# Mixture-of-experts layer: two 64-row expert visits replaced by full 128-row visits of the loop

## What is computed

```python
def moe_swiglu(h, router, w_gate, w_up, w_down):
    probs = softmax(h @ router)
    top_p, top_i = lax.top_k(probs, TOP_K)          # TOP_K = 2
    top_p = top_p / sum(top_p)
    combine = sum(one_hot(top_i, N_EXPERTS) * top_p[..., None])
    a = einsum('bsd,edf->bsef', h, w_gate)          # 8 x 1024 x 1408
    u = einsum('bsd,edf->bsef', h, w_up)            # 8 x 1024 x 1408
    hid = silu(a) * u * combine[..., None]
    return einsum('bsef,efd->bsd', hid, w_down)     # 8 x 1408 x 1024
```

## Time and profile before

| | us |
|---|---|
| median of three runs | 1987.22 |
| the three runs | 1984.53, 1987.22, 1990.09 |
| the profiled execution, its own time | 1985.19 |
| its span in the trace | 1983.4 |

### The profile page before, as it was taken

How to read it: one execution, slowest core, us unless ns; L and a number is a source line. 1 busy time by engine, 2 the same in 40 slices (tenths; PEclk the granted TensorE clock), 3 DMA queues, 4 the chain that set the end, 5 groups by cost and what they waited for, 6 DMA issues and landing times.

```text
span 1983.4 us, 32235 instructions
## 1 busy us (share of the span) xinstructions
PE 1850.1 (93%) x13940; PEld 1553.6 (78%) x13940; DVE 1014.3 (51%) x1302; ACT 797.5 (40%) x1116; POOL 269.0 (14%) x245
## 2 busy tenths in 40 slices
PE   4999899999989999998999899999998989899994
PEld 2889789888878999887888798887877447367884
DVE  1955344454635344326944445545638234157885
ACT  2444632222534322215364522225345243246774
POOL 2510032332000000004400123330002000000001
PEclk9998889999988999998989999999998999999997
DMA  9461142122652334327621223117555986969994
GB/s 343 175 224 49 43 160 94 58 86 86 224 190 89 124 127 127 128 106 275 230 100 48 116 88 108 44 46 253 205 202 182 379 309 240 378 213 320 372 380 151
DMA packets 186386, 350.70 MB, mean 177 GB/s; under 512 B 5097, under 2 KB 60417, under 8 KB 185744
## 3 DMA queue, kind: packets, MB, share of 16 engines
q1 hardware_dynamic: 182464, 335.03, 47.7%
q0 software_dynamic: 3792, 13.77, 2.0%
HBM read 319.41 MB, written 29.36 MB: 176 GB/s over the span
## 4 chain that ended last, share of the span: by engine, by line
PE 81%; DMA 6%; DVE 4%; ACT 4%; SPq 2%; issue 1%; POOL 0%; POOLq 0%; DVEq 0%; ACTq 0%
PE bank L1101 5%; PE bank L1653 5%; PE bank L1622 5%; PE bank L1330 5%; PE bank L1623 4%; PE bank L1625 4%; PE bank L1103 4%; PE bank L1102 4%; PE bank L1513 3%; PE bank L1511 3%; PE bank L1512 3%; PE bank L1137 3%; PE bank L1139 3%; PE bank L1138 3%; PE bank L1055 2%; DMA ring<-in_ada_w 2%
## 5 line engine op out<-in xcount | busy, mean ns | idle before, releaser
L1103 PE MATMUL bank<-hT_hi,ring_split 128*128 128x384 f32 x576 | 195.8, 340 | 0.0
L1759 ACT ACTIVATE ring_split<-ring 128x1024 fp32r<-128x1024 f32 (+2 forms) x84 | 119.5, 1441 | 177.2 <-DMA ring<-in_ffn_w_up 103.8
L2620 DVE TENSOR_TENSOR ring_split<-ring,ring_split 128x2048 fp32r<-128x2048 f32 (+1 forms) x28 | 73.9, 2671 | 141.8 <-ACT ring_split L1759 141.8
L1101 PE MATMUL bank<-hT_hi,ring_split 128*128 128x384 f32 x384 | 142.3, 371 | 4.3 <-DVE modv L2294 2.9
L1139 PE MATMUL bank<-ring_split,hT_hi 128*128 128x256 f32 x480 | 137.2, 286 | 0.0
L720 DVE TENSOR_TENSOR ring_split<-ring,w_upper_a 128x1536 fp32r<-128x1536 f32 (+2 forms) x54 | 96.5, 1814 | 76.3 <-PE bank L1653 68.1
L1102 PE MATMUL bank<-hT_lo,ring_split 128*128 128x384 f32 x384 | 130.4, 340 | 0.0
L1653 PE MATMUL bank<-ring,hT 128*64 128x256 f32 (+1 forms) x592 | 109.7, 510 | 17.9 <-DMA ring<-in_moe_w_up 13.9
L1513 PE MATMUL bank<-hT_hi,ring_split 128*128 128x384 f32 x352 | 118.8, 337 | 0.0
L1511 PE MATMUL bank<-hT_hi,ring_split 128*128 128x384 f32 x352 | 117.6, 334 | 0.0
L1512 PE MATMUL bank<-hT_lo,ring_split 128*128 128x384 f32 x352 | 117.2, 333 | 0.0
(11 more groups left out here) (423 smaller groups left out, 4539.3 us busy)
## 6 DMA issues: line engine op xcount, KB each, us to landing
ring<-in_w_in SPq DMA_DIRECT2D x28, 2048.0 KB, 8.9
ring<-in_ada_w SPq DMA_DIRECT2D x24, 2048.0 KB, 12.8
ring<-in_moe_w_gate SPq DMA_DIRECT2D x32, 1024.0 KB, 7.7
ring<-in_moe_w_up SPq DMA_DIRECT2D x32, 1024.0 KB, 10.0
ring<-in_moe_w_down SPq DMA_DIRECT2D x16, 1536.0 KB, 9.0
ring<-in_w_branch SPq DMA_DIRECT2D x8, 1536.0 KB, 12.8
ring<-in_ffn_w_gate SPq DMA_DIRECT2D x11, 1024.0 KB, 5.4
ring<-in_ffn_w_up SPq DMA_DIRECT2D x11, 1024.0 KB, 7.9
```

The source lines that it names most:

```text
L1101: mm(out, hi, hT_hi[:, k], start=k == 0, stop=False)
L1103: last = mm(out, lo, hT_hi[:, k], start=False, stop=k == KT - 1)
```

## The change

The small visits go. `VISITS` becomes V0 = (0, None), V1 = (1, 0), V2 = (2, 1): every expert has an item of 128 slots, and ranks 1 and 2 have a side of 64 slots besides. Ranks 3 to 7 are items 3 to 7, all in the loop. `N_SIDE` becomes 2, `N_FIX` 8, `NI` 16; `FIRST` stays 3. The loop's body is the same.

Since no small visit stands ahead of a wide one now, slots 0 and 1 of a side are put behind products 8 and 9 of the item visit before it (`wide_next`), in V0 and in V1. V0's load of rows (`rows_load(0)`) fetches the rows of item 1 and of side 0 instead of side 0 alone, and V0 transposes both. The semaphore counts (`slots`, `sides_before`) follow.

The core of the diff:

```diff
-VISITS = ((0, None), (None, 0), (1, 1), (None, 2), (2, 3))
+VISITS = ((0, None), (1, 0), (2, 1))
...
-BY_RANK = ((0, None), (1, 1), (2, 3), (3, None), (4, None), (5, None), (None, 2), (None, 0))
+BY_RANK = ((0, None), (1, 0), (2, 1), (3, None), (4, None), (5, None), (6, None), (7, None))
...
+        def wide_next(v):
+
+            return None not in following(v)
+
+        def sides_before(v):
+
+            return sum(s is not None for _, s in VISITS[:v])
...
         slots = []
-        for item_v, s in VISITS:
+        for v, (item_v, s) in enumerate(VISITS):
+            ahead_v = [(following(v)[1], j) for j in range(2)] if wide_next(v) else []
...
-            elif s is not None:
-                slots += [(s, j) for j in range(2, M_GU + M_DN)]
+            else:
+                slots += ([(s, j) for j in range(2, M_GU + M_DN)] if s is not None else []) + ahead_v
...
+            def rows_load(v):
+
+                n_item, n_side = following(v)
+                if n_item is not None:
+                    sp.wait_ge(ga_mm, 2 * n_item)
+                    sp.dma_start(xs, slot_rows(xslots, n_item)).then_inc(xs_in, 16)
+                if n_side is not None:
+                    if n_side:
+                        sp.wait_ge(side_t, turned("rows", n_side - 1))
+                    side_load(n_side)
...
                 if j == M_SLOT + 1:
                     for done in moved:
                         sp.wait_ge(done, 32)
-                    side_load(0)
+                    rows_load(0)
...
                             if s is not None and j < M_GU + 2:
                                 side_slot(v, j + 2)
+                            elif v is not None and j >= M_GU + 2 and wide_next(v):
+                                side_slot(v + 1, j - M_GU - 2)
...
                         if not last:
                             for j in range(2):
-                                lower(j, i + 1)
+                                lower(j, i + 1, following(v_)[1] if v_ is not None else None)
```

More of the change, by code:

```diff
@@ L646, in build @@
         slots = []
-        for item_v, s in VISITS:
+        for v, (item_v, s) in enumerate(VISITS):
+            ahead_v = [(following(v)[1], j) for j in range(2)] if wide_next(v) else []
             if item_v is None:
-                slots += [(s, j) for j in range(M_GU + M_DN - 1)] + [(s + 1, 0), (s, M_GU + M_DN - 1), (s + 1, 1)]
-            elif s is not None:
-                slots += [(s, j) for j in range(2, M_GU + M_DN)]
+                slots += [(s, j) for j in range(M_GU + M_DN - 1)] + ahead_v[0:1] + [(s, M_GU + M_DN - 1)] + ahead_v[1:2]
+            else:
+                slots += ([(s, j) for j in range(2, M_GU + M_DN)] if s is not None else []) + ahead_v
         def m_place(j, split=False):
@@ L856, in _ @@
                 e = sp.value_load(table[0:1, x:x + 1], min_val=0, max_val=NE - 1)
-                n_item, n_side = following(v)
                 for j in range(M_GU + M_DN):
@@ L867, in _ @@
                             store_out(VISITS[v - 1][0])
[L868 to L873, removed]
+                        rows_load(v)
             with sp.Fori(FIRST, n_items) as i:
@@ L1686, in side_visit @@
                                 side_turn(s, M_BLK - 1)
-                            if j >= M_GU + 2:
+                            if j >= M_GU + 2 and wide_next(v):
                                 side_slot(v + 1, j - M_GU - 2)
@@ L1707, in main_visit @@
                                 pe.wait_ge(side_yt, FG + 2 * N_SIDE)
-                            elif j == 2 and v:
-                                pe.wait_ge(side_yt, FG + 2 * VISITS[v - 1][1] + 2)
+                            elif j == 2 and sides_before(v):
+                                pe.wait_ge(side_yt, FG + 2 * sides_before(v))
                             for h in parts_of(j):
@@ L2176, in side_visit @@
                         gathered(i)
-                        side_rows(n_side)
+                        if n_side is not None:
+                            side_rows(n_side)
                         side_copy(s, 2)
```

## The result

| | before | after |
|---|---|---|
| median, us | 1985.42 (20 runs, 1978.04 to 1991.92) | 1992.6 (20 runs, 1986.28 to 2001.6) |
| ratio of after to before | | 1.0032, 95% interval 1.0021 to 1.0043 |
| span of the profiled execution | 1983.4 | 1999.8 |

The changed kernel is slower by 0.32%, some 6.4 us; the two medians lie 7.2 us apart. The forecast was 1992.5 us, 5.3 us over the 1987.2 us that three runs of the kernel before had given.

The account below looks back on a forecast made before the run. The tensor engine was taken to bound all but the small visits, which were bound by loads. The terms -107.96 + 96.60 + 14.27 + 2.18 + 0.17 = +5.26 us on a 1987.22 us median gave 1992.5 us, range 1986 to 2001.

Parts of the forecast that it names:

- The two visits removed and the two added: Expert stage: dropping small visits V1 and V3 saves 107.96 us; two more loop visits of 48.30 us add 96.60.
- The moved side slots: Ends of V0 and V1: slots 0 and 1 of two sides, four at 3.57 us, nothing hidden, +14.27 us.
- The transposes: V0 and V1: eight more transposes of item rows in each, 1.09 us per group, +2.18 us; copies hidden.
- the list of signs: Expected timeline: loop visits 48.3 us, V1 82.8, V2 74.6, V0 8.3 longer, no PE wait for weights behind V0.
- The seam of V0: SyncE's queue at V0's end: 512 KB of rows instead of 256 delays later loads 1.9 us, yet costs nothing.
- the second rival: End of V0: item rows land late and weights behind them up to 1.9 us late, +4.0 us, 1996.5; chance 0.14.
- The loop's margin: Loop visits: 18.35 MB at 386 GB/s takes 47.5 of 48.3 us, leaving 0.8 us before loads decide.
- the first rival: Five loop visits in a row become bound by their loads, 3.1 us more in each of four, 2004.9 us; chance 0.08.
- The table and the zero fills: Router's item table of 16 entries instead of 15, +0.17 us; one more tile per zero fill taken at nothing.
- the chance of 0.43 for slower: Whole kernel: probability given to a slowdown of over 0.3%, summed from 0.21, 0.08 and 0.14.

Follow-up runs that it names:

- the second pair of profiles: Changed kernel and kernel before, each profiled again without an edit: stage 464.46 us and 459.04 us.
- the slots thinned: Changed kernel with slots 0 and 1 of both sides computing one of four row tiles each: stage 8.3 us shorter.
- The reordered kernel: Changed kernel with SyncE's wait for written rows and its row loads put behind slots 7 and 8 of V0: 2002.68 us, ratio 1.0072.
- the kernel before with the reordered seam: Kernel before with SyncE's wait for written rows and its row loads put behind slots 7 and 8 of V0: 1991.51 us, ratio 1.001.

## Why the prediction was right

**The two visits removed and the two added.** The whole stage was to grow by 5.3 us and grew by 5.9, and by 5.4 in the second pair of profiles. The five loop visits take 48.29 or 48.30 us, as taken from the earlier trace rows. That each part is in its place, and not only their sum, is shown by the kernels with one small visit kept: V3 costs 5.6 us (5.35 by the terms), V1 0.2 (-0.25 by the terms); against the second profile of the kernel before they are 6.2 and 0.8, so each is known to about 1 us.

**The moved side slots.** Taken at 3.57 us each. One of 16 matmuls stands at 3.65 us in V0's end, but the last 0.07 of it lies beside the next work, as in the earlier trace rows. V1 is 82.80 us, the old V2's 74.48 and 8.3 more; the sum wanted 8.23. With the slots thinned they themselves lost 10.3 us, and the stage 8.3.

**The transposes.** Taken at 2.18 us for two groups of eight. Each group is there, 1.04 us in V0. Their copies on ACT and DVE were hidden, as taken. One thing the sum didn't have: in V0 they cover the gap of 0.54 us that stood ahead of L1034, so this part was over-sized by that. The prediction had read PE's 6.5 us of idle time in V0 as all ahead of its second half; 5.9 of them are, and these 0.54, at 1537, are not.

**V0.** Taken 8.2 us longer (8.3 in the list of signs), measured 9.0 in the first profile and 7.9 in the second, whose V0 is this:

```profile
1496.24:1561.87 65.63, 59.40 (x269) 45.43 (x269) 52.84 (x75) 37.54 (x33) 11.14 (x6) 0.92 0.77 278
```

In the six profiles whose V0 is the same it runs from 65.6 to 66.8 us. PE is busy for 58.1 to 60.8 us of that for the same matmuls (58.1 and 58.2 at a granted clock of 0.95, 59.4 to 60.8 at 0.90 to 0.92), and where it is busy for less it waits longer, for DVE's split (7.6 us instead of 6.0) and for weights. The 0.6 us by which the stage is over the forecast is within this spread; the second pair has 0.1 us.

**The seam of V0.** Taken at nothing, with 0.1 us at its tightest. The next expert's slot 0 was to land at 1550.4 with PE coming at 1550.5. Set back by the 10.1 us by which V0 began later, it landed at 1550.2, and PE came at 1551.1. In three of the six profiles with this V0, the second one of the changed kernel among them, PE came first and waited 0.2 to 0.5 us. That is the weights' part of the second rival, at an eighth of its price or less, and the forecast's nothing stands to within 0.5 us. The rows were never near: they had 4.9 us in hand, since the 512 KB landed in 3.6 us here and not in the 9.5 of a full loop visit, from which the rival had its price. The reordered kernel shows what happens when that is used up. How much a further delay of the weights alone would cost was not tested.

**The loop's margin.** Real and narrow, and not passed: 379 to 381 GB/s in the three full visits. The visits' equal length settles it. With 1 MB more per visit it was passed, two visits later than the first rival said. ACT's 0.5 us of waiting for weights, which the prediction put into every visit, stands in one of the three visits before and, with 1.0 us, in one of the four after. By the 358 GB/s of the Trainium skill, "DMA: Bandwidth & Descriptors", Specifications, the visits could not have held 48.3 us; up to 389 GB/s were measured with the added traffic. The same page, under Measured, says that a lone core gets more than that share, up to 425 GB/s, and the trace agrees with that part. By the page, which figure holds depends on whether the neighbouring core is loading too; this kernel runs on one core, and no run here loads two.

**The table and the zero fills.** Too small to be seen in the spans. Of the table the traces show more: DVE's seven operations take 2.06 us from the start of the first to the start of what follows in both profiles before, and 2.14 and 2.12 after. The term of 0.17 us measured 0.06 to 0.08. The zero fills lie ahead of V0, which begins anywhere from 1492.85 (the kernel with more traffic) to 1505.30, and were not tested by themselves.

**The time of the whole.** The median of the changed kernel is 1992.6 us where 1992.5 was predicted. That nearness is partly luck: the median of before is 1985.4 with 20 runs, not the 1987.2 of three, and the ratio gives +6.4 us with an interval of 4.2 to 8.5, not +5.3. The change lies just beyond the 0.3% that the prediction took as the least that can be told from no change, and the forecast put it just within; the chance of 0.43 for slower stood for that.

## What to carry to other kernels

A visit that is bound by its transfers is worth what else its window hides: set its length against the full visit and everything that must find a new place, one window at a time. Here the two removed windows did the same work and one was free to replace (56.5 us against 56.8), the other cost 5.4 (against 51.2); all four are sums of the terms, which the kernels with one visit kept bear out to about 1 us. When a change is worth a few us in 2000, judge it on the stage that it touches, and profile both kernels twice before reading anything from their spans.

## What the runs showed of the hardware

**Weight loads slow the indirect scatters.** The last three of six indirect writes of rows on POOL's queue took 3.7 us to land (median) in the changed kernel with no loads beside them, and 8.7 us in the kernel before with the reordered seam, with two weight loads (1280 and 1536 KB) going out at once. A wait that looked like lost time for the weights was shielding the scatters.

**The time ahead of V0 varies by 12 us.** It is 1492.9 to 1505.3 us, while DVE's busy time ahead of V0 stays at 737.9 to 739.0 us. PE is busy there for 1409.6 to 1422.1 us with the same 11,742 or 11,743 matmuls, at a mean granted clock of 0.97 up to 1414.5 us and 0.96 from 1416.9 on. The rest is idle time of PE, which varies too, from 78.0 to 86.6 us, so the clock alone doesn't give the order: the shortest stretch has 1414.5 us busy, and the one with 1409.6 begins V0 at 1496.2. What brings each drop of the clock was not found.

**A load bound can stay hidden for two visits.** With 1 MB more per visit, at 387 to 389 GB/s, the visits behind the wide one were 48.3, 48.3, 49.7 and 51.7 us long. In the last of these the granted clock also fell to 0.97, and PE's busy time rose by 1.5 us. That filled places carry the first two is argued, not tested.
